# Setup of the state-space filters: wide power steps, products in four 32-row strips, and a later row spread

## The chip, the cores and the metric

The kernel runs on one core of a Trainium2 chip. The metric is the device time in microseconds (us) of one execution, taken as the median of several runs.

## The reference

The program computes two transformer-like blocks on a sequence of 1024 positions of width 1024, all in float32. The change lies in the first block, before its three mixers. What matters of it:

```python
mod = (c @ w_ada[l] + b_ada[l])[:, None, :]
h = rms_norm(x, g_pre_mix[l]) * (1.0 + sc_m) + sh_m
z = h @ w_in[l]
u, f, q, k, v = jnp.split(z, splits, axis=-1)
...
lam_bar = jnp.exp(lam * dt)
b_bar = ((lam_bar - 1.0) / lam)[..., None] * b
states = []
for d, rev in ((0, False), (1, True)):
    bu = lax.complex(jnp.einsum('bsgc,gpc->bsgp', uf, b_bar[d].real),
                     jnp.einsum('bsgc,gpc->bsgp', uf, b_bar[d].imag))
    a = jnp.broadcast_to(lam_bar[d], bu.shape)
    _, h_dir = lax.associative_scan(_scan_combine, (a, bu), reverse=rev, axis=1)
    states.append(h_dir)
h = states[0] + states[1]
y = (jnp.einsum('bsgp,gcp->bsgc', h.real, c_re) - jnp.einsum('bsgp,gcp->bsgc', h.imag, c_im))
```

u is split into 24 groups of 16 columns, each with 64 complex states, and there are two directions. The six rows of `mod` are shifts, scales and gates. The kernel does not scan over 1024 positions. It cuts the sequence into chunks of 8 and needs, for every lag k from 0 to 7, the products lam_bar^k * b_bar (tile `lam_b`), and from them the filter taps C * lam_bar^k * b_bar (`k_sum`) that act inside a chunk; the scan over the 128 chunks runs with lam_bar^8 and its powers (`pw`, from which the table `turn` is built).

## The kernel before, in words

Each engine has a program of its own, written out by hand in program order; the engines meet only at semaphores. `steps.settle()` makes an engine wait for its own earlier instructions. Nothing is scheduled by a planner, so what stands behind a waiting instruction waits too.

**TensorE (L4302 is `unit_step`).** The projection z is made in ten units of 128 columns. A unit is eight steps k of six matmuls (hi*hi, hi*lo, lo*hi in two halves of 512 positions). A unit waits for `win_lo`, VectorE's low part of its weights. Between the steps stand small pieces of other work: `sum_block(b)` (L4231), which adds up the partial products of c and block b of w_ada over the partitions; `turn_state(i)` (L4294), twelve groups of four transposes of `lam_b`; and, behind unit 6, `filters()` (L4283): 48 products with `lam_b` as stationary operand (128 columns) and `c_pad` as moving operand (32 columns). Unit 8 begins by waiting for `k_ready` 2. Behind unit 9 come `spread_row(0)` and `spread_row(1)` (L4242), which lay two modulation rows over all partitions, and then `mix_tensor`: four products (L284), the Fourier products along the heads (L294), the transposes of `u_t` (L307), of `u_rows` (L315) and of v, first scores (L341), state products (L331) and the Fourier products over the positions (L356).

**VectorE.** Its program in this stretch is a list of `split(n)` (L4067, the low part of unit n's weights), `weigh_block(b)` (L4019, L4022: eight multiply-adds of pieces of 128x512 that SyncE's queue loads through four buffers), `lam_step(k)` (one power: `complex_step`, L3974 to L3983, twelve operations of 192 elements), nine calls of `square` (L4090 to L4095, five operations of 24 elements) for `pw`, the work on the taps (L4123 to L4135), `fold_fourier` (L589 to L593), `late_modulations` (L4030 to L4036, the source of the rows to be spread), `turns(0)` (L561 to L581, the rotation table), and `scale_row` (L4044), which multiplies `row_a` and `row_b` with the spread rows and stands between the sixth and the last level of the table. Then `mix_vector` copies `u_rows` (L601) and builds the table of the other direction.

`weigh_block(b)` from block 2 on waits until `sum_block(b - 2)` has run, since two accumulators are used in turn. `weigh_block(6)` so waits for `sum_block(4)`, which stands in unit 8 behind the wait for `k_ready` 2.

**ScalarE** casts the high part of the weights (L3778), copies a finished unit out of PSUM (L3784) and copies the turned states (L3772). **GpSimd** computes `carry_out` (L4172 to L4178); most of it waits for `lam_b_ready`. **SyncE's queue** loads pieces and units in order; in block 5 it waits for `k_ready` 1 before it moves a row of `k_sum` into `k_shift`.

The order around the change, on VectorE:

```python
        split(6)
        for k in range(5, CH):
            lam_step(k)
        split(7)
        weigh_block(4)
        square(pw[:, 0, 1], pw[:, 1, 1], col(12), col(10))
...
        weigh_block(6)
        weigh_block(7)
...
        split(9)
        dve.wait_ge(ada_mm, N_ADA)
        fold_fourier(dve, v, steps)
        late_modulations()
```

Of the kernel before, what the change touches and what calls it, by code (L numbers as in the profile page):

```python
# [15 lines left out]
P = 128  # L16
# [11 lines left out]
CH = 8  # L28
# [33 lines left out]
def body(ctx, nc, a, out):  # L62
# [97 lines left out]
    b_turned, lam_used = lam_turned, dt_spread  # L160
    prm_angle, prm_trig, prm_lam = (sem(n) for n in ("prm_angle", "prm_trig", "prm_lam"))
# [37 lines left out]
    f_diff = place("f_diff", [P, HALF], RR + 10 * KB)  # L199
# [78 lines left out]
    def mix_tensor(pe, t):  # L278

        pe.wait_ge(fw_in, 16 * 5)  # L280
        pe.wait_ge(z_ready, Z_ALL)
# [3 lines left out]
        ins.then_inc(fw_mm, 1)  # L285
        pe.wait_ge(fw_ready, 1)
# [3432 lines left out]
    def _(act):  # L3719
# [120 lines left out]
    def _(dve):  # L3840
# [198 lines left out]
        def scale_row(i):  # L4039

            row = (row_a, row_b)[i]
            dve.wait_ge(k_mm, i + 2)
# [46 lines left out]
        def square(dr, di, sr, si):  # L4089
            steps.add(v.tensor_tensor(col(22), sr, sr, ALU.mult))  # L4090
            steps.add(v.tensor_tensor(col(23), si, si, ALU.mult))
            steps.add(v.scalar_tensor_tensor(col(24), sr, 2.0, si, ALU.mult, ALU.mult))
# [5 lines left out]
        split(2)  # L4098
        weigh_block(0)
        lam_step(1)  # L4100
        split(3)
        weigh_block(1)
        split(4)
        weigh_block(2)
        lam_step(2)
        split(5)
        weigh_block(3)
        lam_step(3)
        lam_step(4)
# [12 lines left out]
        taps = GROUPS * GC  # L4122
        steps.add(v.memset(k_shift[:], 0.0))  # L4123
        dsk = k_sum[0:GC, 0, :].rearrange("c (g o) -> c g o", g=GROUPS)
        steps.add(v.tensor_tensor(dsk, ident[0:GC, 0:GC].unsqueeze(1).to_broadcast([GC, GROUPS, GC]),
                                  dskip_cols[:].unsqueeze(2).to_broadcast([GC, GROUPS, GC]), ALU.mult))
        steps.add(v.tensor_copy(k_sum[:, 1, :], bank(1, taps)))
        steps.settle()
        steps.add(v.tensor_tensor(k_sum[0:GC, 1, :], k_sum[0:GC, 1, :], k_sum[0:GC, 0, :], ALU.add))
        steps.settle()  # L4130
        dve.sem_inc(k_ready, 1)
        split(8)
        weigh_block(5)
        dve.wait_ge(k_shift_in, K_SHIFT_0 + 16)
        v.tensor_tensor(k_sum[:, 0, :], bank(0, taps), k_shift[:], ALU.add).then_inc(k_ready, 1)  # L4135
        weigh_block(6)
        weigh_block(7)
# [8 lines left out]
        def scale_rows():  # L4146
            for i in range(2):
                scale_row(i)

        dve.wait_ge(carry_ready, 2)  # L4150
        turns(v, steps, 0, scale_rows)
# [43 lines left out]
    def _(pe):  # L4195
# [195 lines left out]
```

## Time and profile before

| what | value |
|---|---|
| median of 3 runs | 2918.93 us |
| lowest and highest run | 2916.03 and 2919.35 us |
| span of the profiled execution | 2914.4 us |

No run time of its own is shown for the profiled execution; its span is 4.5 us below the median of the runs, which also hold what lies around the span. The profile names engines PE (TensorE), PEld (its weight loads), DVE (VectorE), ACT (ScalarE), POOL (GpSimd) and SP (SyncE). A product of float32 operands has two records for one matmul of the program, so 48 products of `filters()` are 96 records; a product of the split (fp32r) operands of a unit has one. The stretch that the change touches lies between 77 and 225 us of the span.

### The profile page before, as it was taken

The page shows a single profiled execution, that of the slowest core. Times are in us where ns is not written, and L with a number is a line of the kernel's source. Part 1 is how long each engine was busy: PE and PEld are TensorE (multiplying, and loading weights), DVE is VectorE, ACT ScalarE, POOL GpSimd, SP SyncE. Part 2 cuts the span into 40 slices and gives each one's busy share as a digit, 9 for nine tenths or more (in the row PEclk, how much of TensorE's full clock was granted, in tenths as well). Part 3 has the DMA queues.
Part 4 walks back from the last instruction along what each step waited for, and adds up shares of the span by engine and source line. Part 5 has one row for each costly group of instructions (what it writes and reads, how often), then busy time and mean ns, then how long its engine had stood idle before and what let it go on. Part 6 is the DMA issues. An engine that isn't in the chain of part 4 may idle for free.

```text
span 2914.4 us, 37420 instructions
## 1 busy us (share of the span) xinstructions
PE 2812.8 (97%) x13573; PEld 2252.5 (77%) x13573; DVE 2102.5 (72%) x3839; ACT 1331.9 (46%) x2340; POOL 197.5 (7%) x250
## 2 busy tenths in 40 slices
PE   7998998999999999999999999999999999999997
PEld 3885677788888888888888887786677888888886
DVE  7888727988898568766666667798737866665568
ACT  3113746544444454433333453577744433333443
POOL 2050000000000000000000000223610000000000
PEclk9988999999999999999999999999999999999999
DMA  7542034244445884344447753111023354455864
GB/s 235 152 148 43 9 130 130 83 166 166 162 150 189 278 264 148 130 154 153 151 159 282 252 189 116 50 44 34 1 100 125 130 163 155 151 164 200 299 195 145
DMA packets 345430, 436.84 MB, mean 150 GB/s; under 512 B 29701, under 2 KB 191533, under 8 KB 345070
## 3 DMA queue, kind: packets, MB, share of 16 engines
q1 hardware_dynamic: 342290, 428.46, 45.1%
q10 hardware_dynamic: 2956, 5.99, 0.6%
q8 instruction: 108, 1.77, 0.2%
q14 instruction: 76, 0.62, 0.1%
HBM read 317.59 MB, written 116.50 MB: 149 GB/s over the span
## 4 chain that ended last, share of the span: by engine, by line
PE 72%; DVE 7%; ACT 2%; POOL 1%; issue 1%; DMA 0%; DVEq 0%; SPq 0%; ACTq 0%
PE psum L1993 39%; PE psum L1444 21%; PE psum L2956 4%; PE psum L1984 3%; PE psum L1084 2%; DVE count_junk L3487 1%; PE psum L3159 1%; PE psum L3146 1%; PE psum L3172 1%; PE psum L3036 0%; ACT sign_junk L3253 0%; DVE x_t L1690 0%; DVE x_b L2463 0%; POOL p_wide L3654 0%; DVE x_lo L2536 0%
## 5 line engine op out<-in xcount | busy, mean ns | idle before, releaser
L1444 PE MATMUL psum<-far_op,far_op 128*128 128x512 f32 x2772 | 629.5, 389 | 0.0
L1444 PEld LDWEIGHTS psum<-far_op,far_op 128*128 128x128 f32 x2772 | 520.1, 188 | 108.1 <-issue 0.2
L1993 PE MATMUL psum<-x_b,w_near 128*128 128x512 f32 x1440 | 346.0, 389 | 0.8 <-DVE w_near L1616 0.8
L1993 PE MATMUL psum<-x_t,w_near 128*128 128x512 f32 x1440 | 336.4, 389 | 1.7 <-ACT psum L1730 1.7
L1993 PE MATMUL psum<-x_t,w_far 128*128 128x512 f32 x1440 | 336.3, 389 | 0.0
L1993 PEld LDWEIGHTS psum<-x_t,w_near 128*128 128x128 f32 x1440 | 270.2, 188 | 58.2 <-ACT psum L1730 2.1
L1993 PEld LDWEIGHTS psum<-x_b,w_near 128*128 128x128 f32 x1440 | 270.2, 188 | 57.3 <-issue 1.2
L1993 PEld LDWEIGHTS psum<-x_t,w_far 128*128 128x128 f32 x1440 | 270.2, 188 | 56.3 <-ACT u_keep L1742 0.3
L1208 ACT CAST far_op<-far_a 128x512 fp32r<-128x512 f32 x231 | 143.9, 623 | 316.0 <-PE psum L1444 307.8
L1215 DVE TENSOR_TENSOR far_op<-far_a,far_op 128x512 fp32r<-128x512 f32 x231 | 159.7, 692 | 176.7 <-ACT far_op L1208 175.1
L1993 PE MATMUL psum<-x_b,w_far 128*128 128x512 f32 x720 | 173.1, 389 | 1.7 <-DVE val_row L1862 1.7
L1217 DVE TENSOR_TENSOR far_op<-far_b,far_op 128x512 fp32r<-128x512 f32 x231 | 159.2, 689 | 0.0
L1616 DVE TENSOR_TENSOR w_far<-w_sum,w_far 128x512 fp32r<-128x512 f32 x120 | 82.3, 686 | 106.3 <-ACT w_far L1610 106.3
L1993 PEld LDWEIGHTS psum<-x_b,w_far 128*128 128x128 f32 x720 | 135.1, 188 | 30.1 <-DVE val_row L1862 2.1
L3622 POOL TENSOR_TENSOR split_lo<-raw,split_hi 128x256 fp32r<-128x256 f32 (+1 forms) x60 | 44.8, 781 | 1619.3 <-ACT split_hi L2972 1619.3
L1209 ACT CAST far_op<-far_b 128x512 fp32r<-128x512 f32 x231 | 142.1, 615 | 0.0
L1610 ACT CAST w_far<-w_sum 128x512 fp32r<-128x512 f32 x120 | 73.9, 616 | 119.0 <-PE psum L1993 119.0
L1616 DVE TENSOR_TENSOR w_near<-w_sum,w_near 128x512 fp32r<-128x512 f32 x120 | 80.9, 687 | 64.8 <-ACT w_near L1610 64.7
L1610 ACT CAST w_near<-raw 128x512 fp32r<-128x512 f32 (+1 forms) x129 | 82.8, 642 | 72.3 <-PE psum L1993 61.3
L1616 DVE TENSOR_TENSOR w_far<-raw,w_far 128x512 fp32r<-128x512 f32 (+1 forms) x66 | 47.2, 715 | 88.7 <-ACT w_far L1610 88.7
L1061 DVE TENSOR_TENSOR src_lo<-yc_t,src_hi 128x512 fp32r<-128x512 f32 x31 | 21.4, 692 | 119.1 <-ACT w_out_hi L1054 119.1
L1984 PE MATMUL psum<-x_b,w_near 128*128 128x512 f32 x360 | 91.3, 402 | 8.5 <-DVE x_b L2301 4.1
(534 smaller groups left out, 4826.7 us busy)
## 6 DMA issues: line engine op xcount, KB each, us to landing
far_a<-row_ops SPq DMA_DIRECT2D x231, 256.0 KB, 2.9
row_ops<-hidden SPq DMA_DIRECT2D x99, 512.0 KB, 5.2
raw<-in_ffn_w SPq DMA_DIRECT2D x88, 512.0 KB, 4.4
col_sums<-hidden SPq DMA_DIRECT2D x66, 512.0 KB, 5.6
far_b<-col_sums SPq DMA_DIRECT2D x132, 256.0 KB, 3.6
raw<-in_w_up SPq DMA_DIRECT2D x44, 512.0 KB, 3.8
hidden<-in_ffn_w SPq DMA_DIRECT2D x44, 512.0 KB, 5.1
far_b<-in_ffn_w SPq DMA_DIRECT2D x66, 256.0 KB, 3.3
```

Of the source, the lines that this page charges most:

```text
L1084: ins = t.matmul(bank(2 * n + c), l[:, P * n:P * (n + 1)], r[:, HALF * c:HALF * (c + 1)], start=(first and m == 0), stop=(last and m == 2))
L1208: s.copy(far_a_hi[slot][:], far_a[late][t % FB][:]).then_inc(f_hi, 1)
L1209: s.copy(far_b_hi[slot][:], far_b[late][t % FB][:]).then_inc(f_hi, 1)
L1215: v.tensor_tensor(far_a_lo[slot][:], far_a[late][t % FB][:], far_a_hi[slot][:], ALU.subtract).then_inc(f_lo, 1)
L1217: v.tensor_tensor(far_b_lo[slot][:], far_b[late][t % FB][:], far_b_hi[slot][:], ALU.subtract).then_inc(f_lo, 1)
L1444: ins = t.matmul(bank(b + n), l[slot][:, rows], r[slot][:], start=(fresh and i == 0 and m == 0), stop=(i == FH - 1 and m == 2), skip_group ...
L1610: nc.scalar.copy(op_parts(p, i)[0], op_source(p, i)).then_inc(op_hi, 1)
L1616: nc.vector.tensor_tensor(lower, op_source(p, i), upper, ALU.subtract).then_inc(op_lo, 1)
L1984: ins = t.matmul(bank(b), at[:, l, cols], r, start=(first and m == 0), stop=(last and m == 2))
L1993: ins = t.matmul(bank(b), at[:, l, cols], x[:, k, r], start=(start and k == 0 and m == 0), stop=(k == 3 and m == 2), skip_group_check=not ...
L2956: ins = t.matmul(bank(2 * slot + half)[0:m], l[:, P * k:P * k + m], r[:, k, HALF * half:HALF * (half + 1)], start=(k == 0 and i == 0), sto ...
L3622: ins = g.tensor_tensor(tile_of(w_rest, m)[:, k:k + 2], tile_of(raw[slot], m)[:, k:k + 2], tile_of(w_top, m)[:, k:k + 2], ALU.subtract)
```

## The change

1. `lam_step` handles both directions in one operation: six operations of 384 elements for twelve of 192. All seven steps are kept, and the order of splits, blocks and steps is new: the first step now stands ahead of `split(2)`.
2. `square` writes its imaginary part directly and squares both parts in one operation: three operations for five (four in the first call). The nine squares move ahead of `split(7)` and `weigh_block(4)`.
3. `filters()` swaps its operands: `c_pad` is stationary (32 columns) and `lam_b` moving (128 columns), and the four products of a group write four strips of 32 PSUM partitions. It moves from behind unit 6 into unit 6, ahead of step 2.
4. The result lies turned, so ScalarE copies it to `k_sum` (two copies), and `turn_filters()` in unit 6 ahead of step 6 turns it back with six transposes. VectorE's tap work waits for that.
5. `split(9)` moves ahead of `weigh_block(7)`; `sum_block(7)` moves from step 0 to step 2 of unit 9, and `sum_block(5)` in unit 8 from step 2 to step 3. The wait for all sums behind `split(9)` is left out here (`late_modulations` has its own), and `f_diff` moves to another address.
6. The two `spread_row` stand behind the first products of `mix_tensor`, and both `scale_row` behind the whole of `turns(0)`.

```diff
-    def mix_tensor(pe, t):
+    def mix_tensor(pe, t, spread_row):
         pe.wait_ge(fw_in, 16 * 5)
-        pe.wait_ge(z_ready, Z_ALL)
+        pe.wait_ge(z_ready, Z_ALL - 1)
...
         ins.then_inc(fw_mm, 1)
+        for i in range(2):
+            spread_row(i)
         pe.wait_ge(fw_ready, 1)
...
+            if n == 7:
+                act.wait_ge(k_mm, 1)
+                for d in range(2):
+                    nc.scalar.copy(k_sum[:, d, :], bank(d, GROUPS * GC)).then_inc(taps_copied, 1)
...
         def lam_step(k):
-            complex_step(lam_b_at(k), lam_b_at(k - 1), 13, 14)
+            re, im = spread_both(13), spread_both(14)
+            by = [w_tmp[:, i // 2, 2 * (i % 2):2 * (i % 2) + 2] for i in range(4)]
+            for ri in range(2):
+                steps.add(v.tensor_tensor(by[2 * ri], lam_b_both(k - 1, ri), re, ALU.mult))
+                steps.add(v.tensor_tensor(by[2 * ri + 1], lam_b_both(k - 1, ri), im, ALU.mult))
+            steps.settle()
+            steps.add(v.tensor_tensor(lam_b_both(k, 0), by[0], by[3], ALU.subtract))
+            steps.add(v.tensor_tensor(lam_b_both(k, 1), by[1], by[2], ALU.add))
+            steps.settle()
...
+                steps.add(v.tensor_tensor(prm[:, 22:24, :], both, both, ALU.mult))
+            steps.add(v.scalar_tensor_tensor(di, sr, 2.0, si, ALU.mult, ALU.mult))
             steps.settle()
             steps.add(v.tensor_tensor(dr, col(22), col(23), ALU.subtract))
-            steps.add(v.tensor_copy(di, col(24)))
             steps.settle()
...
+        lam_step(1)
+        for b in range(4):
+            split(2 + b)
+            weigh_block(b)
+            lam_step(2 + b)
         split(6)
-        for k in range(5, CH):
+        for k in range(6, CH):
             lam_step(k)
+        square(pw[:, 0, 1], pw[:, 1, 1], col(12), col(10))
+        for src, dst in ((1, 2), (2, 0)) + tuple((m, m + 1) for m in range(6)):
+            square(pw[:, 0, dst], pw[:, 1, dst], pw[:, 0, src], pw[:, 1, src], pw[:, :, src])
         split(7)
         weigh_block(4)
-        square(pw[:, 0, 1], pw[:, 1, 1], col(12), col(10))
-        square(pw[:, 0, 2], pw[:, 1, 2], pw[:, 0, 1], pw[:, 1, 1])
-        square(pw[:, 0, 0], pw[:, 1, 0], pw[:, 0, 2], pw[:, 1, 2])
-        for m in range(6):
-            square(pw[:, 0, m + 1], pw[:, 1, m + 1], pw[:, 0, m], pw[:, 1, m])
-        dve.wait_ge(k_mm, 1)
+        first_taps()
         split(8)
         weigh_block(5)
+        last_taps()
         weigh_block(6)
+        split(9)
         weigh_block(7)
...
-        split(9)
-        dve.wait_ge(ada_mm, N_ADA)
         fold_fourier(dve, v, steps)
         late_modulations()
...
         def filters():
             pe.wait_ge(lam_b_ready, 1)
             for d in range(2):
-                for q in range(PAIRS):
+                for third in range(PAIRS // 4):
                     for ri in range(2):
-                        ins = t.matmul(bank(d, 2 * GC, 2 * GC * q), lam_b[:, ri, d, q].rearrange("p s c -> p (s c)"),
-                                       c_pad[:, ri, q].rearrange("p e c -> p (e c)"), start=(ri == 0), stop=(ri == 1))
+                        for s in range(4):
+                            q = 4 * third + s
+                            ins = t.matmul(bank(d, P, P * third)[2 * GC * s:2 * GC * (s + 1)],
+                                           c_pad[:, ri, q].rearrange("p e c -> p (e c)"),
+                                           lam_b[:, ri, d, q].rearrange("p s c -> p (s c)"), start=(ri == 0), stop=(ri == 1))
+            ins.then_inc(k_mm, 1)
+        def turn_filters():
+            for d in range(2):
+                pe.wait_ge(taps_copied, TAPS_0 + d + 1)
+                for third in range(PAIRS // 4):
+                    ins = t.transpose(bank(d, P, P * third), k_sum[:, d, P * third:P * (third + 1)], ident[:])
             ins.then_inc(k_mm, 1)
...
+                elif n == 6 and k == 2:
+                    filters()
+                elif n == 6 and k == 6:
+                    turn_filters()
+                elif n == 8 and k in (0, 3, 6):
                     if k == 0:
                         pe.wait_ge(k_ready, 2)
+                    sum_block(4 + k // 3)
+                elif n == 9 and k == 2:
                     sum_block(7)
```

How it moves instructions, at two places. On TensorE, before, at the seam of units 6 and 7 (`psum<-x_hi,win_upper` and the like are a unit's steps, `c_pad,lam_b` the filters):

```order
L4302 MATMUL psum<-x_hi,win_upper_107 128x512 x2
L4302 MATMUL psum<-x_lo,win_upper_107 128x512 x2
L4302 MATMUL psum<-x_hi,win_lower_109 128x512 x2
L4283 MATMUL psum<-c_pad,lam_b 128x32 x48
L4302 MATMUL psum<-x_hi,win_upper_108 128x512 x2
```

and of the change, in unit 6 from `sum_block(3)` on:

```order
L4251 MATMUL psum<-one_cols,ada_acc_77 128x1 x4
L4332 MATMUL psum<-x_hi,win_upper_107 128x512 x2
L4332 MATMUL psum<-x_lo,win_upper_107 128x512 x2
L4332 MATMUL psum<-x_hi,win_lower_109 128x512 x2
L4305 MATMUL psum<-lam_b,c_pad 32x128 x48
L4332 MATMUL psum<-x_hi,win_upper_107 128x512 x2
```

The 48 products now stand ahead of six of unit 6's eight steps; the first number of the shape is now the number of PSUM partitions written, 32 for 128.

On VectorE, the stretch behind the last power step, before (L3983 ends the last step, L4067 is `split(7)`, L4019 begins `weigh_block(4)`):

```order
L3983 TENSOR_TENSOR lam_b<-w_tmp 128x12x16
L4067 TENSOR_TENSOR win_lower_110<-win_raw_106,win_upper_108 128x1024
L4019 TENSOR_SCALAR ada_acc_76<-ada_piece_72,c_cols 128x512
```

and of the change:

```order
L4075 TENSOR_TENSOR lam_b<-w_tmp 128x2x12x16
L4114 TENSOR_TENSOR prm<-prm 128x24
L4115 TENSOR_TENSOR prm<-prm 128x24
L4118 SCALAR_TENSOR_TENSOR pw<-prm 128x24
L4120 TENSOR_TENSOR pw<-prm 128x24
L4117 TENSOR_TENSOR prm<-pw 128x48
L4118 SCALAR_TENSOR_TENSOR pw<-pw 128x24
L4120 TENSOR_TENSOR pw<-prm 128x24
```

The squares now follow the last power step, ahead of `split(7)`, and the tap work stands directly behind `weigh_block(4)`.

## Rows read from the trace of the kernel before

**Rows 1.** The page's first line: the span of the profiled execution.
```profile
span 2914.4 us, 37420 instructions
```

**Rows 2.** Waits of VectorE, 77 to 225 us: total, times, longest (us).
```profile
DVE ada_acc L4022 <- DMA ada_piece<-in_w_ada: 9.6, 18, 1.8
DVE win_lower L4067 <- ACT win_upper L3778: 3.4, 2, 2.8
...
DVE f_diff L589 <- PE psum L4231: 1.1, 1, 1.1
```

**Rows 3.** Timeline, TensorE: start, us, engine line, operation, tiles [idle before it].
```profile
225.42 1.31 PE L307 MATMUL psum<-ident,u_t 128*128 128x128 f32 x8 [2.26 <-DVE u_rows L601]
```

**Rows 4.** Timeline, VectorE: rotation table begins; first copy into u_rows.
```profile
205.61 0.07 DVE L561 MEMSET turn<- 128x12 f32 x1
...
224.68 0.69 DVE L601 COPY u_rows<-psum 128x512 f32<-128x512 f32 x1
```

**Rows 5.** Timeline, TensorE: unit 6, filters, unit 7, start of unit 8.
```profile
138.38 0.72 PE L4302 MATMUL psum<-x_hi,win_upper 128*128 128x512 f32 x2
...
148.04 16.54 PE L4283 MATMUL psum<-c_pad,lam_b 128*128 128x32 f32 x96
...
164.39 1.20 PE L4302 MATMUL psum<-x_hi,win_upper 128*128 128x512 f32 x2
...
169.59 0.62 PE L4302 MATMUL psum<-x_hi,win_upper 128*128 128x512 f32 x2
...
179.66 0.50 PE L4231 MATMUL psum<-one_cols,ada_acc 128*128 128x1 f32 x4
```

**Rows 6.** Timeline, VectorE: power steps, squares, and what follows them.
```profile
112.10 0.36 DVE L3974 TENSOR_TENSOR w_tmp<-lam_b,prm 128x192 f32<-128x192 f32 x1
...
115.58 1.22 DVE L4067 TENSOR_TENSOR win_lower<-win_raw,win_upper 128x1024 fp32r<-128x1024 f32 x1
...
142.24 0.35 DVE L3983 TENSOR_TENSOR lam_b<-w_tmp 128x192 f32<-128x192 f32 x1
...
151.92 0.26 DVE L4090 TENSOR_TENSOR prm<-prm 128x24 f32<-128x24 f32 x1
...
165.68 0.38 DVE L4123 MEMSET k_shift<- 128x384 f32 x1
```

**Rows 7.** Timeline, VectorE: six operations of 384 elements, and the next.
```profile
235.08 0.56 DVE L575 TENSOR_TENSOR turn_tmp<-carry,pw 128x384 f32<-128x384 f32 x1
...
238.14 0.56 DVE L575 TENSOR_TENSOR turn_tmp<-carry,pw 128x384 f32<-128x384 f32 x1
```

**Rows 8.** Timeline, VectorE: last_taps' addition and weigh_block(6).
```profile
176.88 0.56 DVE L4135 TENSOR_TENSOR k_sum<-psum,k_shift 128x384 f32<-128x384 f32 x1
...
180.65 0.63 DVE L4019 TENSOR_SCALAR ada_acc<-ada_piece,c_cols 128x512 f32<-128x512 f32 x1 [3.21 <-PE psum L4231]
```

**Rows 9.** Timeline, TensorE: spread rows; state products on two 64-column strips.
```profile
212.36 3.73 PE L4242 MATMUL psum<-ident,row_cols 128*128 128x128 f32 x32
...
215.93 0.28 PE L284 MATMUL psum<-fw_rows,dft_d 128*128 128x128 f32 x1
...
237.10 1.53 PE L331 MATMUL psum<-u_chunk,state_in 128*64 128x128 f32 x24
...
238.56 14.00 PE L356 MATMUL psum<-dft_w,f_mixed 128*128 128x512 f32 x32
```

**Rows 10.** Windows of 2 us: busy us of each engine, granted clock (PEclk), DMA.
```profile
152.00:154.00 2.00, 2.00 (x14) 2.00 (x13) 1.90 (x10) 0.00 (x0) 1.84 (x5) 0.60 0.99 365
...
168.00:170.00 2.00, 2.00 (x7) 1.63 (x6) 1.89 (x3) 0.00 (x0) 2.00 (x3) 0.63 0.05 12
```

**Rows 11.** Timeline: ScalarE's cast of unit 8; GpSimd's chain, first and last.
```profile
154.06 1.04 ACT L3778 CAST win_upper<-win_raw 128x1024 fp32r<-128x1024 f32 x1 [15.69 <-DMA win_raw<-in_w_in]
...
142.79 1.53 POOL L4172 TENSOR_TENSOR e_tmp<-carry_out,prm 128x192 f32<-128x192 f32 x1 [97.54 <-DVEq L4055]
...
189.97 1.04 POOL L4178 TENSOR_TENSOR carry_out<-e_tmp 128x192 f32<-128x192 f32 x1
```

More of the change, by code:

```diff
@@ L198, in body @@
     yf_odd = place("yf_odd", [P, 2, HALF], XR + 28 * KB)
-    f_diff = place("f_diff", [P, HALF], RR + 10 * KB)
+    f_diff = place("f_diff", [P, HALF], RR + 16 * KB)
     u_rows = place("u_rows", [P, GROUPS, CH, GC], RR)
@@ L4041, in scale_row @@
             row = (row_a, row_b)[i]
-            dve.wait_ge(k_mm, i + 2)
+            dve.wait_ge(k_mm, i + 3)
             dve.wait_ge(bc_in, 16 * 3)
@@ L4087, in _, with square @@
                 split(1)
[L4089 to L4092, printed above, removed]
+        def square(dr, di, sr, si, both=None):
+            if both is None:
+                steps.add(v.tensor_tensor(col(22), sr, sr, ALU.mult))
+                steps.add(v.tensor_tensor(col(23), si, si, ALU.mult))
+            else:
+                steps.add(v.tensor_tensor(prm[:, 22:24, :], both, both, ALU.mult))
+            steps.add(v.scalar_tensor_tensor(di, sr, 2.0, si, ALU.mult, ALU.mult))
@@ L4093, in square, with first_taps @@
             steps.settle()
             steps.add(v.tensor_tensor(dr, col(22), col(23), ALU.subtract))
-            steps.add(v.tensor_copy(di, col(24)))
             steps.settle()
-        split(2)
-        weigh_block(0)
-        lam_step(1)
[L4101 to L4109, printed above, removed]
+        taps = GROUPS * GC
+        def first_taps():
+            dve.wait_ge(k_mm, 2)
+            steps.add(v.memset(k_shift[:], 0.0))
+            dsk = k_sum[0:GC, 0, :].rearrange("c (g o) -> c g o", g=GROUPS)
+            steps.add(v.tensor_tensor(dsk, ident[0:GC, 0:GC].unsqueeze(1).to_broadcast([GC, GROUPS, GC]),
+                                      dskip_cols[:].unsqueeze(2).to_broadcast([GC, GROUPS, GC]), ALU.mult))
+            steps.add(v.tensor_copy(k_sum[:, 1, :], bank(1, taps)))
+            steps.settle()
+            steps.add(v.tensor_tensor(k_sum[0:GC, 1, :], k_sum[0:GC, 1, :], k_sum[0:GC, 0, :], ALU.add))
+            steps.settle()
+            dve.sem_inc(k_ready, 1)
@@ L4110, in _, with last_taps @@
+        def last_taps():
+            dve.wait_ge(k_shift_in, K_SHIFT_0 + 16)
+            v.tensor_tensor(k_sum[:, 0, :], bank(0, taps), k_shift[:], ALU.add).then_inc(k_ready, 1)
+        lam_step(1)
+        for b in range(4):
+            split(2 + b)
+            weigh_block(b)
+            lam_step(2 + b)
         split(6)
-        for k in range(5, CH):
+        for k in range(6, CH):
             lam_step(k)
+        square(pw[:, 0, 1], pw[:, 1, 1], col(12), col(10))
+        for src, dst in ((1, 2), (2, 0)) + tuple((m, m + 1) for m in range(6)):
+            square(pw[:, 0, dst], pw[:, 1, dst], pw[:, 0, src], pw[:, 1, src], pw[:, :, src])
@@ L4125, in _ @@
[L4125 to L4131, printed above, removed]
+        first_taps()
         split(8)
         weigh_block(5)
-        dve.wait_ge(k_shift_in, K_SHIFT_0 + 16)
@@ L4135, in _ @@
-        v.tensor_tensor(k_sum[:, 0, :], bank(0, taps), k_shift[:], ALU.add).then_inc(k_ready, 1)
+        last_taps()
         weigh_block(6)
+        split(9)
         weigh_block(7)
@@ L4140, in _ @@
         dve.sem_inc(fw_zero, 1)
-        split(9)
-        dve.wait_ge(ada_mm, N_ADA)
         fold_fourier(dve, v, steps)
         late_modulations()
-        def scale_rows():
-            for i in range(2):
-                scale_row(i)
         dve.wait_ge(carry_ready, 2)
-        turns(v, steps, 0, scale_rows)
+        turns(v, steps, 0)
+        for i in range(2):
+            scale_row(i)
         mix_vector(dve, v, steps)
@@ L4333, in _ @@
             ins.then_inc(win_mm, 1)
-            if n == 6:
-                filters()
-        for i in range(2):
-            spread_row(i)
-        mix_tensor(pe, t)
+        mix_tensor(pe, t, spread_row)
 def constants():
```

13 lines of the change are left out of this document (7 added, 6 removed).

## The prediction

> **What bounds the kernel now.** I took the span first [rows 1]: 2914.4 us, 4.5 us below the median of the runs (2918.93). The sum below is a difference inside the span; I take it off the median, as if the 4.5 us around the span stayed. A measurement of this kernel can tell about 0.2% from no change, 5.8 us here. Then I read the waits of VectorE from 77 to 225 us [rows 2], and the timelines of both engines there. VectorE waits little: 9.6 us in total for pieces of w_ada, 3.4 us for ScalarE's casts (one wait of 2.8, one of 0.6), 3.2 us for TensorE ahead of `weigh_block(6)` [rows 8], 1.1 us for `sum_block(7)`. At the end of the stretch TensorE waits for VectorE: 2.26 us at the transposes of `u_t`, until VectorE has finished the rotation table and made its first copies into `u_rows` [rows 3, 4]. So the date on which the mixers start is VectorE's 224.68, and TensorE's filters (16.35 us, 148.04 to 164.39 [rows 5]) count only because they delay `sum_block(4)` at 179.66 [rows 5], for which `weigh_block(6)` waits until 180.65 [rows 8]. The question is thus how much shorter VectorE's list gets, and whether TensorE is early enough at unit 8.
>
> **VectorE up to k_ready 2.** (a) The first power step moves into the idle 2.8 us ahead of `split(2)` [rows 2]: 2.8 saved. (b) A power step takes 3.48 us now (112.10 to 115.58 [rows 6]). Six operations of 384 elements take 3.06 us, settles included (235.08 to 238.14 [rows 7]). Seven steps save 7 x 0.42 = 2.9. (c) The nine squares take 13.76 us for 45 operations (151.92 to 165.68 [rows 6]), 0.306 each while GpSimd works beside them. The new ones have 4 + 8 x 3 = 28 operations. At the same price, since GpSimd then works too, 8.6 us: 5.2 saved. If the time went with the elements instead of the operations, at least the dropped copies (9 of 45) would go, 2.8 saved; that is the low end. (d) `lam_step(3)` and the others stand between blocks, so pieces and casts have time to land: the 0.6 us wait for a cast goes, and of the longest wait for a piece (1.8 us [rows 2]) I take 1.0. Together 1.6, bounds 0.6 and 2.6. (e) Against it: the cast of unit 8 waits for its load [rows 11], and the load is issued behind the fourth piece of `weigh_block(4)`. That block began right behind `split(7)`, 142.59 + 1.3 = 143.9; it now begins 1.3 us later (below), so the cast starts at 155.4 and ends at 156.4. VectorE, at its taps at 165.68 - 12.5 = 153.2 and through with them 2 us later, waits 1.1 us. Sum: 2.8 + 2.9 + 5.2 + 1.6 - 1.1 = 11.4, so `last_taps`, which ended at 177.44 [rows 8], ends at 166.0.
>
> **TensorE up to unit 8.** The last power is ready at 142.59 - 2.8 - 2.9 - 1.6 = 135.3 [rows 6]. Squares (8.6) and `split(7)` (1.2) then put `weigh_block(4)` at 145.1. A unit's step takes (148.04 - 138.38) / 7 = 1.38 us [rows 5], so unit 6 reaches its step 2 at 139.8: the filters don't wait, with 4.5 us to spare. What they take, F, no row shows. The spread rows, 128 moving columns on the whole array, take (215.93 - 212.36) / 32 = 0.112 us a record. The state products, 128 columns on two strips of 64, take (238.56 - 237.10) / 24 = 0.061 [rows 9]: there two strips run beside each other. For 96 records that gives 10.7 us if the four new strips take turns, 5.8 at the pitch of two strips, 2.9 if four strips halve it again. I take 4.4, between the last two, since L331 is the nearest row and its strips are twice as wide. The Trainium skill, in TensorEngine Tiling (Array Packing), section Overview, gives up to a fourfold speedup for an operand side of 32 or less; as an estimate by that page F would be 2.7 us, and no row here has four strips. The six transposes cost at most 6 x 0.112 = 0.7. ScalarE copies the result while unit 6 goes on; between filters and transposes lie four steps, 5.5 us, so neither waits, and the transposes end at 146.0 + F, ahead of VectorE's 153.2. Unit 7 takes 15.27 us now (164.39 to 179.66), but its first twelve records take 5.2 us (164.39 to 169.59) where two steps take 2.76 [rows 5]: the granted clock was half there (0.60 in the window at 152, still 0.63 at 168 [rows 10]). Without that it is 12.8. So TensorE reaches unit 8 at 148.04 + F + 0.7 + 12.8 = 161.5 + F, 165.9 with my F, just as `k_ready` 2 comes at 166.0.
>
> **From there on.** (f) `weigh_block(6)` now waits only for `sum_block(4)` behind `last_taps`, about 1.1 us (a group of `sum_block` plus two semaphores; it was 0.99 from 179.66 to 180.65) where it waited 3.2: 2.1 saved. (g) `split(9)` stands ahead of `weigh_block(7)` and `sum_block(7)` runs behind `fold_fourier`'s start, so the 1.1 us wait goes [rows 2]. The scaling of the rows only changes its place on VectorE, 2.8 us either way, and its source is early: TensorE needed 36.3 us from unit 8's start to the end of the spread (179.66 to 215.93 [rows 5, 9]); from 166.1 that ends at 202.4 at the latest, and VectorE comes to it at 207.3. GpSimd's chain took 48.2 us (142.79 to 191.01 [rows 11]) from the last power on; it would end at 183.5, and the table starts at 205.61 - 14.6 = 191.0 [rows 4]. Both covers gone, each microsecond more would count in full. The three products ahead of the spread and the later wait for `z_ready` lie on TensorE under the same cover: nothing. SyncE's queue waits for `k_ready` 1 with the second half of block 5's pieces behind it; that signal comes 2 us after 153.2 where it came 2 us after 165.68, and the first of those pieces needs a buffer that `weigh_block(5)` frees only later: no price. Sum: 11.4 + 2.1 + 1.1 = **14.6 us**; VectorE's first copy into `u_rows` moves from 224.68 to 210.1, TensorE waits about 5 us there, and what follows moves as a block. 2918.9 - 14.6 = **2904.3**.
>
> **Rivals.** *A, the strips take turns.* F = 10.7, TensorE is at unit 8 at 172.2, 6.2 us after `k_ready` 2: gain 8.4, 2910.5. For it: a strip's products use all 128 rows. Against it: L331's pitch. The Trainium skill (TensorE: Matmul & The Clock Gate, Part 3) says that weight loads overlap running matmuls only where the row group differs. By that rule these loads would stand between the products, which leads to A or somewhat beyond; the trace disagrees as far as L331's products, which also span all rows, go at half the pitch of L4242's. *B, the clock.* It fell some 4 us into the old filters and came back 5.2 us after unit 7 began [rows 5, 10]. If it falls inside the new ones, F grows to about 6.5 and the next steps lose 5.2 - 2.76 = 2.4 again: arrival 170.4, 4.4 late, gain 10.2, 2908.7. Denser products and a shorter stretch speak against it. *C, slower.* The wide operations read and write `lam_b` with one dimension more. If that doubled their price (6 x 0.95 + 0.2 = 5.9 us a step), seven steps would cost 17 us more than now instead of 2.9 less, the filters would wait in unit 6, and the gain of 14.6 turns into -5.3: 2924.2. It decides from 3.06 + 14.6 / 7 = 5.1 us a step. L575's 384 elements, with two strided dimensions and a repeated operand, speak against it. *D, absorbed.* The mixers from 225 us on are paced by something that doesn't move, or TensorE's longer pause leaves its clock low for the position products (14.0 us [rows 9]), and at least 9 of the 14.6 us are given back: about 2914. No load there is issued at a fixed time, so I see no mechanism for the whole.
>
> **How the numbers follow.** Forecast 0.60 (own range 2902 to 2907, from the ends of (c) and (d) and F up to 5.8, which costs 1.3), A 0.15, B 0.12, D 0.07, C 0.06. The range 2901.5 to 2911.5 holds the first three and leaves out C and most of D. Faster by over 0.2%: 0.60 + 0.15 + 0.12 = 0.87. Within: D, 0.07. Slower: 0.06.
>
> **What would show it.** Filters of about 4 us inside unit 6 and no stall ahead of them; power steps of 3.1 us; squares of 8 to 9 us; `weigh_block(6)` starting near 167 after a wait of about 1 us; the first copy of `u_rows` near 210 and a wait of TensorE of about 5 us ahead of it. I am wrong if a power step exceeds 5 us, if TensorE arrives at unit 8 later than VectorE's 166 by more than a few us, or if the distance from the first `u_rows` copy to the end of the span changes by more than 3 us.

## The result, and the profile after

| | changed kernel | before, in the same runs |
|---|---|---|
| median | 2904.79 us | 2917.48 us |
| ratio, 95% interval | 0.9947 [0.9932, 0.9962] | |
| profiled execution, span | 2898.9 us (its time 2900.72) | 2914.4 us |
| median of a second series (6 runs) | 2909.04 us | 2916.64 us |
| ratio, 95% interval | 0.9967 [0.9955, 0.9979] | |

The kernel is faster by 0.3% to 0.5%. Of the first series one of four runs (6694.56 us) was disturbed; it is left out of the ratio, but the median of 2904.79 counts it, and that of the three others is 2902.88. So the gain is 14.6 us by the undisturbed runs of the first series (12.7 by its medians as they stand) and 7.6 us by the second. The profile shown is of the fastest of all these runs. The second series has a profile of its own (span 2907.0, from a run of 2908.8, near its series' median), and both are read below. Line numbers are those of the changed kernel: L4026 and L4029 are `weigh_block`, L4090 `split`, L4071 to L4075 a power step, L4114 to L4120 a square, L4251 `sum_block`, L4305 `filters`, L4314 `turn_filters`.

The page's first line and VectorE's waits from 77 to 215 us (total, times, longest), answering to [rows 1, 2]:

```profile
span 2898.9 us, 37375 instructions
```
```profile
DVE ada_acc L4029 <- DMA ada_piece<-in_w_ada: 7.4, 17, 1.1
DVE ada_acc L4026 <- PE psum L4251: 1.4, 1, 1.4
```

The waits for casts (3.4 us) and for `sum_block(7)` (1.1) are gone, the one ahead of `weigh_block(6)` is 1.4 for 3.2. VectorE's timeline, answering to [rows 4, 6, 8] (start, us, engine line, operation, tiles, idle before):

```profile
75.82 0.55 DVE L4071 TENSOR_TENSOR w_tmp<-lam_b,prm 128x384 f32<-128x384 f32 x1
...
78.29 0.55 DVE L4075 TENSOR_TENSOR lam_b<-w_tmp 128x384 f32<-128x384 f32 x1
...
133.25 0.18 DVE L4114 TENSOR_TENSOR prm<-prm 128x24 f32<-128x24 f32 x1
...
144.35 1.48 DVE L4090 TENSOR_TENSOR win_lower<-win_raw,win_upper 128x1024 fp32r<-128x1024 f32 x1
...
154.06 0.38 DVE L4128 MEMSET k_shift<- 128x384 f32 x1 [0.26 <-DVE ada_acc L4029]
...
156.24 1.31 DVE L4090 TENSOR_TENSOR win_lower<-win_raw,win_upper 128x1024 fp32r<-128x1024 f32 x1
...
165.94 0.56 DVE L4141 TENSOR_TENSOR k_sum<-psum,k_shift 128x384 f32<-128x384 f32 x1
...
167.92 0.69 DVE L4026 TENSOR_SCALAR ada_acc<-ada_piece,c_cols 128x512 f32<-128x512 f32 x1 [1.42 <-PE psum L4251]
...
191.37 0.07 DVE L564 MEMSET turn<- 128x12 f32 x1
...
210.46 1.29 DVE L604 COPY u_rows<-psum 128x512 f32<-128x512 f32 x2
```

The first power step begins at 75.82 and what follows it at 78.88, so it takes 3.06 us. The squares run from 133.25 to 144.35, `last_taps` adds at 165.94, `weigh_block(6)` begins at 167.92, the table at 191.37, and the first copy into `u_rows` comes at 210.46 where it was 224.68. TensorE, answering to [rows 3, 5, 9]:

```profile
138.50 2.83 PE L4305 MATMUL psum<-lam_b,c_pad 128*32 128x128 f32 x96
141.26 0.74 PE L4332 MATMUL psum<-x_hi,win_upper 128*128 128x512 f32 x2
...
166.75 1.12 PE L4251 MATMUL psum<-one_cols,ada_acc 128*128 128x1 f32 x8 [3.04 <-DVE k_sum L4141]
...
211.20 3.62 PE L310 MATMUL psum<-ident,u_t 128*128 128x128 f32 x16 [3.94 <-DVE u_rows L604]
...
223.25 3.27 PE L359 MATMUL psum<-dft_w,f_mixed 128*128 128x512 f32 x7
```

The filters take 2.76 us (138.50 to 141.26) where they took 16.35, without a stall ahead of them.

What kept the old ones busy can be read from the rows of the weight loads (PEld), before and after, and from two windows of before (us, PE, PEld, VectorE, ScalarE, GpSimd, granted clock, DMA share, GB/s):

```profile
147.82 16.62 PEld L4283 LDWEIGHTS psum<-c_pad,lam_b 128*128 128x128 f32 x96
```
```profile
148.00:150.00 2.00, 2.00 (x20) 1.96 (x19) 1.52 (x3) 0.00 (x0) 1.92 (x3) 1.00 0.87 266
156.00:158.00 2.00, 2.00 (x12) 2.00 (x11) 1.93 (x8) 0.02 (x1) 1.92 (x5) 0.50 0.03 9
```
```profile
138.50 2.56 PEld L4305 LDWEIGHTS psum<-lam_b,c_pad 128*32 128x32 f32 x96 [0.36 <-issue]
```

The loads of 128 columns filled the old filters from end to end, 19 of them in 2 us at full clock and 11 at half. At the full clock's pace 96 would take some 10.1 us (an estimate: 96 x 2.00 / 19), so of the 13.6 us saved some 6 are the low clock and some 7 the form.

At unit 8 TensorE now waits 3.04 us for VectorE. The granted clock of the changed kernel in windows of 2 us, beside [rows 10]:

```profile
138.00:140.00 2.00, 2.00 (x59) 1.64 (x61) 1.90 (x6) 0.00 (x0) 1.84 (x5) 1.00 0.00 0
140.00:142.00 2.00, 2.00 (x54) 1.70 (x44) 1.86 (x6) 0.60 (x2) 1.92 (x5) 1.00 0.00 0
...
212.00:214.00 2.00, 2.00 (x10) 1.53 (x10) 1.48 (x3) 0.00 (x0) 0.00 (x0) 0.50 0.00 0
...
216.00:218.00 2.00, 1.76 (x15) 1.30 (x13) 1.83 (x15) 1.45 (x3) 0.00 (x0) 1.00 0.76 300
```

It stays full under the new filters. Behind TensorE's wait for `u_rows` it is at half, and back at full by 216.

**The second profile.** Its waits over the same stretch, rows of VectorE and of TensorE, and one window:

```profile
DVE ada_acc L4029 <- DMA ada_piece<-in_w_ada: 9.3, 20, 1.3
DVE ada_acc L4026 <- DMA ada_piece<-in_w_ada: 2.3, 1, 2.3
```
```profile
144.89 1.48 DVE L4090 TENSOR_TENSOR win_lower<-win_raw,win_upper 128x1024 fp32r<-128x1024 f32 x1
...
155.12 0.38 DVE L4128 MEMSET k_shift<- 128x384 f32 x1 [0.26 <-DVE ada_acc L4029]
...
169.58 0.83 DVE L4026 TENSOR_SCALAR ada_acc<-ada_piece,c_cols 128x512 f32<-128x512 f32 x1 [2.33 <-DMA ada_piece<-in_w_ada]
...
194.31 0.07 DVE L564 MEMSET turn<- 128x12 f32 x1
```
```profile
214.17 3.88 PE L310 MATMUL psum<-ident,u_t 128*128 128x128 f32 x16 [6.14 <-DVE u_rows L604]
...
228.00 4.56 PE L359 MATMUL psum<-dft_w,f_mixed 128*128 128x512 f32 x10
```
```profile
218.00:220.00 2.00, 1.22 (x7) 1.17 (x7) 1.81 (x13) 0.02 (x1) 0.00 (x0) 0.50 0.44 78
```

The same instructions, but 11.6 us of waits for pieces of w_ada where the first had 7.4 (before: 10.1, of which [rows 2] show 9.6). Ahead of `weigh_block(6)` it is a piece that comes last, not TensorE, and the clock is still at half at 218 to 220. Its D starts at 136.72, and its first `u_rows` copy comes at 213.42.

**Where the time went.** To compare runs whose start-up differs by a microsecond, I call D the distance from `sum_block(3)` in unit 6 (TensorE, 137.57 before, 136.12 and 136.72 after) to the first `u_rows` copy. The start of D, before and in the first profile, and then the saving, us:

```profile
137.57 0.95 PE L4231 MATMUL psum<-one_cols,ada_acc 128*128 128x1 f32 x8
```
```profile
136.12 0.95 PE L4251 MATMUL psum<-one_cols,ada_acc 128*128 128x1 f32 x8
```

| piece, up to | before | predicted saving | first profile | second |
|---|---|---|---|---|
| end of the last power step | 5.0 behind the start of D | 7.3 | 7.9 | 7.9 |
| the squares | 13.76 | 5.2 | 2.7 | 2.7 |
| `split(7)`, `weigh_block(4)` | 9.3 | 0 | -0.4 | -0.9 |
| taps to the sum of `last_taps` | 11.2 | -1.1 | -0.7 | -0.4 |
| start of `weigh_block(6)` | 3.8 | 2.1 | 1.8 | 0.9 |
| start of the table | 25.0 | 1.1 | 1.5 | 0.2 |
| first `u_rows` copy | 19.1 | 0 | 0.0 | 0.0 |
| **D** | 87.1 | **14.6** | **12.8** | **10.4** |
| ahead of D | | 0 | 1.5 | 0.9 |
| `u_rows` copy to the position products (L359) | 13.88 | 0 | 1.1 | -0.7 |
| from there to the end | 2675.8 | 0 | 0.2 | -3.2 |
| **span** | 2914.4 | 14.6 | 15.5 | 7.4 |

### The profile page after: what moved, and what is told of

Read it like the earlier page. It is cut to its first block, busy times and chain, and to the rows that moved or that the text cites. A ratio compares the mean times of both kernels' runs of the same rounds, so it can differ in the third digit from the quotient of the medians.

```text
span 2898.9 us, 37375 instructions
## 1 busy us (share of the span) xinstructions
PE 2794.9 (96%) x13579; PEld 2235.2 (77%) x13579; DVE 2099.6 (72%) x3780; ACT 1333.0 (46%) x2342; POOL 200.6 (7%) x250
## 4 chain that ended last, share of the span: by engine, by line
PE 72%; DVE 7%; ACT 2%; POOL 1%; issue 1%; DMA 0%; DVEq 0%; SPq 0%; ACTq 0%
PE psum L1996 39%; PE psum L1447 21%; PE psum L2959 4%; PE psum L1987 3%; PE psum L1087 2%; DVE count_junk L3490 1%; PE psum L3162 1%; PE psum L3149 1%; PE psum L3175 1%; PE psum L3039 0%; ACT sign_junk L3256 0%; DVE x_t L1693 0%; DVE x_b L2466 0%; POOL p_wide L3657 0%; DVE x_lo L2539 0%
```

## Experiments

The first four undo or do one part alone; the others ask what limits the stretch now. "One run" is one profiled run, with one time. The changed kernel's own two profiles differ by 2.4 us in D, so one profile leaves D uncertain by some 2 us. Before had a median of 2919.1 us beside the first four kernels, 2918.9 beside the next four, 2916.64 beside the second series of the changed kernel and the two kernels that follow it here, and 2917.75 beside the last.

**The filters in their old form.** The changed kernel, with 128x32 products as before, at their new place, without `turn_filters` and ScalarE's copies:

```diff
-                elif n == 6 and k == 6:
-                    turn_filters()
...
-                        for s in range(4):
-                            q = 4 * third + s
+                for q in range(PAIRS):
+                    for ri in range(2):
+                        ins = t.matmul(bank(d, 2 * GC, 2 * GC * q), lam_b[:, ri, d, q].rearrange("p s c -> p (s c)"),
```

> The changed kernel with the old form of the filter products (48 products, lam_b stationary, 32 moving columns, no transposes, no copies), but at the new place in unit 6; VectorE's new list is kept. Measure: D, the time from TensorE's sum_block(3) in unit 6 to VectorE's first copy into u_rows (87.11 us before the change, 74.34 with it). My theory says both parts are needed: TensorE comes to unit 8 about 42 us after sum_block(3) as before, weigh_block(6) waits for sum_block(4), and D is about 85.6 (11 us of the gain lost, about 2915 us in all). Rival 'VectorE's shorter list alone is the gain': D stays within 1 us of 74.3.

2913.89 us median, ratio 0.9985 [0.9976, 0.9994]; D 84.8. TensorE's and VectorE's rows of it:

```profile
138.57 16.74 PE L4299 MATMUL psum<-c_pad,lam_b 128*128 128x32 f32 x96
```
```profile
166.86 1.51 DVE L4086 TENSOR_TENSOR win_lower<-win_raw,win_upper 128x1024 fp32r<-128x1024 f32 x1 [9.17 <-ACT win_upper L3781]
...
179.33 0.49 DVE L4022 TENSOR_SCALAR ada_acc<-ada_piece,c_cols 128x512 f32<-128x512 f32 x1 [2.38 <-PE psum L4247]
```

VectorE is nearly as early here as in the changed kernel (at `split(8)` by 157.69, where the second profile has 157.29), and then stands 9.17 us. ScalarE can't cast unit 8's weights until unit 6 has been computed, and unit 6 holds the 16.7 us of filters. D came out as I expected, but the large wait is this one, and not the one at `weigh_block(6)` that I had named, which is 2.4. Without the new filters VectorE's whole part of the change is worth 2.3 us of D.

**The new filters alone**, in the kernel before (unit 6 ahead of step 2, with copies and transposes):

```diff
+                elif n == 6 and k == 2:
+                    filters()
+                elif n == 6 and k == 6:
+                    turn_filters()
...
             ins.then_inc(win_mm, 1)
-            if n == 6:
-                filters()
```

> The kernel before with only the new filter products, their copies and transposes, at the new place in unit 6; VectorE's list is the old one. Rival 'the gain is TensorE's 13.6 us (16.35 us of filters became 2.76)': D falls from 87.1 to about 73.5. My theory: TensorE is early at unit 8, waits there some 13 us for k_ready 2, which comes 39.9 us after sum_block(3) as before, and only the wait of weigh_block(6) shrinks from 3.2 to 1.4 us: D about 85.3, gain about 2 us (2917).

2918.85 us, ratio 1.000 [0.999, 1.001]; D 88.0.

```profile
141.52 2.83 PE L4290 MATMUL psum<-lam_b,c_pad 128*32 128x128 f32 x96 [2.47 <-DVEq L4060]
```
```profile
180.59 0.48 DVE L4024 TENSOR_SCALAR ada_acc<-ada_piece,c_cols 128x512 f32<-128x512 f32 x1 [2.22 <-DMA ada_piece<-in_w_ada]
```

TensorE saves its 13.6 us and none of it reaches the end: `weigh_block(6)` waits for a piece instead, 2.22 where it waited 3.21 for TensorE, and VectorE's taps came 1.6 us later within D; of that 1.3 are the squares, which took 15.05 us here for 13.76 with the same 45 operations. D is 2.7 us above the 85.3 that I expected. So each half alone is stopped by the engine that the other half speeds up.

**Narrow power steps** (twelve operations of 192 elements, in the new places).

```diff
-            for ri in range(2):
-                steps.add(v.tensor_tensor(by[2 * ri], lam_b_both(k - 1, ri), re, ALU.mult))
...
+            complex_step(lam_b_at(k), lam_b_at(k - 1), 13, 14)
```

> The changed kernel with the power steps in twelve operations of 192 elements. Theory (the list adds up one to one): seven steps at 3.48 instead of 3.06 us, D 74.3 + 2.9 = 77.2. Rival (waits for pieces of w_ada absorb it): D below 75.5.

One run: 2911.51 us, D 79.95. Against the second profile of the changed kernel (76.7), which has about the same waits for pieces (11.6 us; 11.5 here), that is 3.3 more, where the sum had 2.9; against the first it is 5.6.

**The old squares** (45 operations), in the new place.

```diff
-            steps.add(v.scalar_tensor_tensor(di, sr, 2.0, si, ALU.mult, ALU.mult))
             steps.settle()
             steps.add(v.tensor_tensor(dr, col(22), col(23), ALU.subtract))
+            steps.add(v.tensor_copy(di, col(24)))
```

> The changed kernel with the old squares (five operations) at their new place. If a square's price is by the operation at the 0.396 us that the new ones showed: 45 x 0.396 = 17.8 us instead of 11.1, D about 81. If the new ones only saved the nine dropped copies and the wide ones cost more each: 13.8 us as before, D about 77.0.

One run: 2910.42 us, D 80.2. The squares took 14.15 us (135.21 to 149.36) for 11.1 in the changed kernel: 3.1 us for the form, not 5.2. That is 0.314 us for each of 45 operations where the 28 new ones take 0.396, so the price isn't one per operation either. D is 3.5 above the second profile.

**GpSimd's chain later.** GpSimd resumes `carry_out` only behind the squares. One edit, made by a second signal:

```diff
+        dve.sem_inc(lam_b_ready, 1)
         split(7)
         weigh_block(4)
...
-        pool.wait_ge(lam_b_ready, 1)
+        pool.wait_ge(lam_b_ready, 2)
```

> The changed kernel; GpSimd resumes its carry_out chain only behind the nine squares (11 us later) instead of with them. Theory: the squares cost 11.1 us instead of about 4 because GpSimd works beside them; alone they take 9 x 0.42 = 3.8 us (by the pitch of the first levels of the rotation table), so 7 us go. GpSimd's chain (50 us) then ends about when the rotation table wants to start, costing 0 to 2 us. D about 68 to 69 (2898 us). Rival: the price of a small operation is its own latency, GpSimd has no part in it: squares still near 11 us, and the later chain delays the table, D 76 or more.

2906.35 us, ratio 0.996 [0.9947, 0.9974]; D 77.7. Its squares, first and last row, and its waits:

```profile
135.76 0.18 DVE L4114 TENSOR_TENSOR prm<-prm 128x24 f32<-128x24 f32 x1
...
136.39 0.21 DVE L4117 TENSOR_TENSOR prm<-pw 128x48 f32<-128x48 f32 x1
136.52 0.17 DVE L4118 SCALAR_TENSOR_TENSOR pw<-pw 128x24 f32<-128x24 f32 x1
136.72 0.18 DVE L4120 TENSOR_TENSOR pw<-prm 128x24 f32<-128x24 f32 x1
...
140.94 1.23 DVE L4090 TENSOR_TENSOR win_lower<-win_raw,win_upper 128x1024 fp32r<-128x1024 f32 x1
```
```profile
DVE turn L564 <- POOLq L4212: 4.2, 1, 4.2
DVE ada_acc L4026 <- PE psum L4252: 2.6, 1, 2.6
```

And the same three operations in the changed kernel, with GpSimd beside them:

```profile
136.86 0.41 DVE L4117 TENSOR_TENSOR prm<-pw 128x48 f32<-128x48 f32 x1
137.18 0.53 DVE L4118 SCALAR_TENSOR_TENSOR pw<-pw 128x24 f32<-128x24 f32 x1
137.75 0.44 DVE L4120 TENSOR_TENSOR pw<-prm 128x24 f32<-128x24 f32 x1
```

Alone the squares take 5.18 us, beside GpSimd 11.1: an operation of 0.18 us becomes one of 0.4 to 0.5. The Trainium skill (SBUF — State Buffer, section Who interferes with whom) says that a VectorE instruction with two inputs in SBUF contends with a GpSimd instruction that reads SBUF; these rows fit that. I had expected 3.8 us for the squares and a D of 68 to 69. The 5.9 us don't arrive: VectorE now waits 4.2 us at the table for GpSimd's chain, and 2.6 for TensorE at `weigh_block(6)`.

**GpSimd's chain earlier** (it resumes behind the first power step, and so runs beside the others).

```diff
-            if k == CH - 1:
+            if k in (1, CH - 1):
                 dve.sem_inc(lam_b_ready, 1)
```

> The changed kernel; GpSimd resumes its chain already behind the first power step (about 79 us). Theory of interference: squares near 4 us, weigh blocks 4 to 6 some 0.7 us shorter each, but the power steps 2 to 5 run beside GpSimd and go from 3.06 to about 6 us each: D about 79 to 81, slower than the changed kernel. Rival (no interference): D 74.3.

One run: 2911.97 us. The second power step now takes 4.79 us (89.09 to 93.88) beside GpSimd, `sum_block(3)` comes at 139.55 (3 us later), and the filters wait 2.5 us for the last power and take 4.4:

```profile
144.50 4.44 PE L4305 MATMUL psum<-lam_b,c_pad 128*32 128x128 f32 x96 [2.50 <-DVEq L4078]
```
```profile
144.00:146.00 2.00, 1.50 (x30) 1.37 (x34) 1.72 (x10) 0.00 (x0) 0.00 (x0) 0.61 0.00 0
146.00:148.00 2.00, 2.00 (x45) 1.84 (x40) 1.72 (x12) 0.00 (x0) 0.00 (x0) 0.53 0.00 0
```

The same 96 records took 2.76 us at full clock; here the granted clock is 0.61 and 0.53. GpSimd ended at 138.44, ahead of the squares, and they took 5.06 us: short when GpSimd comes later and short when it is done before, so it is its work beside them that makes them long. D is 76.7, less than I expected, but the first `u_rows` copy comes at 216.28, 3 to 6 us later than in the changed kernel.

**sum_block(4) in unit 7**, so that it doesn't stand behind the wait for `k_ready` 2; `last_taps` waits for it.

```diff
+                elif n == 7 and k == 2:
+                    sum_block(4)
...
-                    if k == 0:
+                    if k == 3:
                         pe.wait_ge(k_ready, 2)
```

> The changed kernel with sum_block(4) in unit 7, ahead of its step 2, and the wait for k_ready 2 ahead of step 3 of unit 8. The 3.0 us that TensorE waits at unit 8 and the 1.4 us that weigh_block(6) waits both go. Theory: only VectorE's wait counts, D 74.34 - 1.4 = 72.9. Rival 'TensorE's wait counts': D 71.3.

One run: 2902.15 us, D 76.1, where I expected 72.9. The wait for TensorE is gone, and one of 1.9 us for a piece stands in its place. If anything was gained, one run can't show it.

**Spread and scaling back in the middle of the table** (part 6 of the change undone).

```diff
-        mix_tensor(pe, t, spread_row)
+        for i in range(2):
+            spread_row(i)
+        mix_tensor(pe, t, lambda i: None)
...
-        turns(v, steps, 0)
-        for i in range(2):
-            scale_row(i)
+        turns(v, steps, 0, lambda: [scale_row(i) for i in range(2)])
```

> The changed kernel with the spread rows back at the end of unit 9 and their scaling back in the middle of the rotation table. Theory: the place is worth at most the wait at the scaling, since TensorE ends the spread at about 201 and VectorE comes to it at 200.9: D 74.3 to 75.

One run: 2905.22 us, D 77.2, half a microsecond above the second profile and 2.9 above the first. My 74.3 to 75 went by the first profile alone. A price of the place can't be told from the kernel's own variation; none is seen against the second profile.

**The changed kernel again**, because the variants had 9 to 12 us of waits for pieces.

> The changed kernel itself, once more, to learn how far the stretch from unit 6's sum_block(3) to the first u_rows copy varies by itself: 74.3 us in its first profile, with only 7.4 us of waits for pieces of w_ada, where the variants of it had 9 to 12. Theory: the first profile was a lucky one, and this one has 76 us and 9 us of waits for pieces, the time 2904.8 as its median. Rival: 74.3 again, and the variants' 76 to 78 are their own edits' doing.

2909.04 us, ratio 0.9967 [0.9955, 0.9979]; D 76.7, pieces 11.6 us. The first profile was a lucky one, and the time was 4.2 us worse than I expected.

**Both: the chain later and sum_block(4) in unit 7.**

> Two edits together: GpSimd's chain resumes only after the squares (they take 5 us alone, not 11), and sum_block(4) stands in unit 7 (so that weigh_block(6) doesn't wait for TensorE). Theory: GpSimd's chain of 54 us now ends at 195, so what VectorE gains by 190 is waited for again at the rotation table's start, some 4 us: 76 to 77 us for the stretch, the time within 1.5 us of the changed kernel. Rival (the table can hide it): 71, the time 4 us less.

2906.13 us, ratio 0.996 [0.9947, 0.9972]; D 77.6. Counted from the start of D, `weigh_block(6)` begins 5.3 us earlier than in the second profile, but the table at 58.5 us, where the second profile has 57.6: 3.3 us are waited for GpSimd, and 12.3 for pieces. I had expected the wait at the table, some 4 us; D is above my 76 to 77, and the median is 2.9 us below the changed kernel's beside the same runs of before, with intervals that overlap.

**As that, and three steps of the chain early,** at 44 to 57 us, where GpSimd had been idle until 133:

```diff
-        for k in range(2, 5):
+        for k in range(2, 8):
             carry_step(0, k)
-        pool.wait_ge(lam_b_ready, 1)
-        for k in range(5, CH + 1):
+        pool.wait_ge(lam_b_ready, 2)
+        for k in range(8, CH + 1):
```

> As the one with both edits, and GpSimd takes three more steps of its chain early, at 44 to 54 us, where it idled until 133, so that after the squares only 8 steps of 11 are left and end near 169. Theory: the squares take 5 us, the stretches after 169 run without GpSimd beside them, nothing waits for GpSimd at the table: 70 to 72 us for the stretch, less up to 1.5 us given back at 44 to 54 (more if VectorE's normalisation there suffers): the time 2900 to 2902. Rival (what is gained is waited for at the pieces of w_ada, which land on their own clock, waits for pieces 12 us and more): 75 us, the time as the changed kernel's.

2903.62 us, ratio 0.9947 [0.9935, 0.996], beside 2909.04 for the changed kernel on the same chip, both against the same runs of before. The gain over the changed kernel is 5.4 us, though the time is above my 2900 to 2902. D is 69.7, the smallest of all. Its rows:

```profile
44.98 3.76 DVE L3843 TENSOR_SCALAR x_rows<-x_rows,stat_b 128x1024 f32<-128x1024 f32 x4
...
188.81 0.07 DVE L564 MEMSET turn<- 128x12 f32 x1
```
```profile
208.65 3.88 PE L310 MATMUL psum<-ident,u_t 128*128 128x128 f32 x16 [4.54 <-DVE u_rows L604]
```

Nothing waits for GpSimd at the table, which starts at 188.81. The early steps have a price: the normalisation's four operations take 3.76 us where they took 2.74, and `sum_block(3)` comes at 138.19, 1.5 us later than in the second profile. I had the chain's end too early: 169, where it is 184.7.

**Three steps early, alone.** To see which of the three edits pays:

```diff
-        for k in range(2, 5):
+        for k in range(2, 8):
...
-        for k in range(5, CH + 1):
+        for k in range(8, CH + 1):
```

> The changed kernel with one edit: GpSimd takes three more steps of its chain early, at 44 to 54 us; the rest of it still starts where the wide steps end and so runs beside the squares, and sum_block(4) stays in unit 8. It ends near 175, not 184. Theory (the gain of the version with three edits, 7 us of the stretch, comes mostly of the squares being alone): 11 us for the squares again, 1 to 2 us less in the rows at the table's start, 75 us for the stretch, the time within 2 us of the changed kernel's 2905 to 2909. Rival (it comes of the chain's early end): 70 to 71 us with slow squares all the same, the time 2903 to 2904.

2908.91 us, ratio 0.9972 [0.996, 0.9983]; D 74.9, squares 11.07, the chain's end 173.2, but `sum_block(3)` only at 140.06. What is won in D is lost ahead of it. So the gain of the version with three edits needs the squares alone **and** a chain that is done when the table starts. With only the first, `turn` waits for GpSimd; with only the second, the squares stay at 11 us. Whether the third edit, `sum_block(4)` in unit 7, has a part in it isn't known: the other two weren't run without it. Why the same early steps cost 3.3 us ahead of D here and 1.5 there isn't settled.

## Why the prediction held, and where it didn't

**Time.** Forecast 2904.3 (range 2901.5 to 2911.5), measured 2904.8 and 2909.0. The first is closer than the reasons deserve, by luck. Of the 15.5 us of its profile 12.8 are the stretch, 1.5 lay ahead of anything that had changed (TensorE's first unit began at 55.11 for 56.59), and 1.1 came at TensorE behind `u_rows`, where its clock was back at full 4 us behind the wait and not some 9. The second shows 10.4 us from the stretch and 3.2 lost past 228 us. So 14.6 us was too much for the mechanism by 2 to 4 us. The mechanism itself held: VectorE's list sets the date, and it gets shorter only if TensorE does too. The own range of 2902 to 2907 doesn't follow from its ends: those of (c), (d) and F, added up, give 2903.3 to 2909.0.

**(a), (b), (d): power steps and idle time.** 7.9 us saved for a predicted 7.3. A step takes 3.06 us, as [rows 7] had it. Rival C (steps above 5.1 us) is out.

**(c): the squares, mis-sized.** "At the same price, since GpSimd then works too, 8.6 us": they take 11.1. 28 operations at 0.396 us each, not 0.306. This is the mis-sized term of the sum: it saved 2.7 of 5.2 us, just under the low end (2.8) that I had kept. What the old price hid is that an operation's time here isn't its own: alone it is 5.18 / 28 = 0.185, and the rest is GpSimd. The 28 that are left lose 5.9 us to it; the price per operation of a mixture doesn't carry over when its parts change.

**(e): the wait for the cast of unit 8 didn't come.** ScalarE's row:

```profile
154.50 1.05 ACT L3781 CAST win_upper<-win_raw 128x1024 fp32r<-128x1024 f32 x1 [12.25 <-DMA win_raw<-in_w_in]
```

The cast began 8.7 us behind the start of `weigh_block(4)` (145.76), where I had 10.3, and ended at 155.55; VectorE came to `split(8)` at 156.24, 10.5 us behind that start, where I had 10.1. So it was mainly the load that I had put too late. It was worth 1.1 us in the kernel's favour. In the same places, though, VectorE lost 1.1 to 1.3 us in all (table) for which the sum had nothing. Only part of that are pieces: the waits for them in blocks 4 and 5 were 1.3 us before and 1.5 and 1.9 in the two profiles. Most of the rest are longer operations, such as `split(7)` at 1.48 us for 1.23; why they were longer isn't shown, since GpSimd worked beside them before as well.

**(f), (g): weigh_block(6) and block 7.** 1.8 and 1.5 us in the first profile for 2.1 and 1.1; in the second 0.9 and 0.2. The wait for TensorE shrank as forecast, and in the second profile a piece took its place: what is late there is the DMA, for which I had a term only up to unit 7.

**F, and rivals A and B.** The filters took 2.76 us, 0.029 a record, where I took 4.4. The four strips run beside each other, so A is out. The Trainium skill (TensorE: Matmul & The Clock Gate, Part 3) has the rule that weight loads overlap running matmuls only where the row group differs. The trace disagrees: these products all span 128 rows, and their loads were busy for 2.56 of the 2.76 us while the products ran. The granted clock stayed 1.00 under them, so B didn't come; with the chain earlier the filters did run at a low clock, and took 4.4 us, so B's 6.5 was too high. The error cost nothing: TensorE was at unit 8 3.04 us ahead of VectorE, where I had them level.

**D, absorbed.** The first profile has u_rows to the end within 1.3 us of before; the second is 3.9 us longer, beyond the 3 us that I had set as the mark of being wrong. But the new filters alone have the `u_rows` copy where before has it (224.60) and 2679.7 us from the position products to the end, 3.9 us more than before. Over the 14 profiles that part lies between 2673.7 and 2679.7 without a clear relation to the arrival: the earliest arrival (207.9) has 2675.2, the latest (224.68) 2675.8. That it is chance and no absorption is what this suggests; it isn't proved.

**Covers.** GpSimd's chain ended at 184.5, 7 us ahead of the table, as forecast (183.5 and 191.0). This cover was the one to watch: with the chain resumed behind the squares it was gone, at a wait of 4.2 us. The move of the spread and of the scaling was forecast to cost nothing; one run with it undone shows no difference beyond the kernel's own.

## What to carry to other kernels

When two engines alternate in front of one date, cost both halves together and each alone: here the new filters alone gave nothing and the rest without them 4 to 5 us (ratio 0.9985), the two together 8 to 15. A price per operation read beside a second engine is that pair's price; look whether the neighbour works on the same memory at that time, and whether its work can be moved into idle time *and* still be done when it is wanted. And measure how far the kernel varies by itself before reading a difference of 2 us out of one profile.

## What the runs showed of the hardware

- Four strips of 32 columns, 128 rows each, float32: 96 records of 128 moving columns in 2.76 us, 0.029 us each, against 0.061 on two strips and 0.112 on the whole array [rows 9]. That is at full clock; at a granted clock of 0.5 to 0.6 the same 96 took 4.4 us.
- 96 float32 products of 32 moving columns with 128x128 weights: the weight loads filled the stretch, 19 in 2 us at full clock and 11 at half.
- Operations of 24 to 48 elements with inputs in SBUF take 0.185 us in a row alone, and 0.396 beside GpSimd's operations of 192 elements; the whole series 5.06 to 5.18 us in four profiles and 11.0 to 11.1 in seven.
- A tensor-scalar operation of 1024 elements in place, with one tile as input, went from 2.74 to 3.76 us for four when GpSimd worked beside it (3.53 with the three early steps alone).
- With the same instructions, waits for the pieces of w_ada came to 7.4 us in one profile and 11.6 in another, and `weigh_block(6)` waited for TensorE in the one and for a piece in the other.
- TensorE's clock was at half behind its wait for `u_rows`, until 216 us in the first profile (4 us of wait) and still at 218 to 220 in the second (6 us of wait). Before, a wait of 2.3 us was followed by half clock until 234, so the length of the wait doesn't tell how long it stays low.
